# Expert layers: float32 gather and scatter without a second part, the third tile on halves of TensorE, weights in runs of 8 KB

## The chip, the cores and the metric

The program runs on one core of a Trainium2 chip. The metric is the device time of one execution in microseconds (us), of which the kernel before has a median of 965.29 us in three runs (964.44 to 967.16). The traces are of one profiled execution each.

## What is computed

A trunk of two layers runs over 320 tokens of width 1024: 256 of a prompt and 64 of eight samples. Layer 0 has a pooling mixer, layer 1 a sparse attention whose keys and values are projected after layer 0; each layer ends with a mixture of experts. The change is in the experts and in how weights lie in memory. Of 16 experts in 4 groups each token gets 2, of the group that its router picks:

```python
def hmoe(xn, r_group, r_expert, w_gu, w_down):
    ...
    for e in range(N_EXPERTS):
        gu = x2 @ w_gu[e]                                # 1024 x 1024
        hdn = jax.nn.silu(gu[:, :D_EXPERT]) * gu[:, D_EXPERT:]
        y = y + comb[:, e:e + 1] * (hdn @ w_down[e])     # 512 x 1024
```

All weights are float32: 6 MB for an expert, 96 MB for the 16 of a layer.

## The kernel before, in words

The 320 tokens lie in three tiles of 128, 128 and 64 rows (TILE_ROWS) in `H`, the residual stream. Each expert has 64 slots (CAP). Work goes by pairs of experts, 8 pairs to a layer, and by batches of 8 experts (4 pairs), two to a layer.

- `ffn_front` makes the router's tables and the normed rows. ACT writes them rounded to float32r (`copy_high`), DVE the rest that the rounding left (`low_part`, L726): one tile in the front, two at the start of `moe`. The rest of the third tile lies in the upper 64 rows of its high part. At the end PE multiplies constants to stay busy (`keep_streaming`, L217), and all engines meet.
- `gather(b, c)` (L949) is TensorE's: for each of 8 chunks of 128 columns, five products of 512 columns (two parts of tile 0, two of tile 1, one of tile 2 with both parts) against the 0/1 matrix `SG` that DVE builds in one step (L1152). ACT copies each result to `XS` (L1092). Three PSUM banks take turns, and chunk c + 2 follows the gate-up products of step c.
- `gate_up(e)` (L967): 8 steps of 2 products on the two column halves of the array. `turn_hidden` (L981) and `turn_scatter` (L993) transpose; `down(p)` (L1007) has 32 products for the pair, of which the second 16 wait for the last two weight units.
- ACT weighs the product of down by the slots' weights into float32r (`down_high`, L1119), DVE makes what the rounding left (`down_low`, L1174). `scatter(p, m)` (L1033) has six steps of two products (high and low), and DVE adds each to `H` (`add_sums`, L1183). Steps 0 to 3 of pair p lie in the gate-up of the odd expert of the pair behind it, steps 4 and 5 between the two `turn_hidden` of that pair. Of the last pair all six come behind `down`.
- Weights come in units of 1 MB (256 rows), 12 to a pair (8 gate-up, 4 down), 96 to a layer, into a ring of 17. SP issues them in order (`load_unit`, L489), unit n when unit n - 17 was used up. In layer 1, 10 units are loaded long before and 7 at the start of the front. In layer 0 SP waits for the store of a hidden piece (L300) ahead of the unit at 109.87 us. Behind the 96 units of layer 0 come 6 MB of `w_kv` (L913) for the projection (L1407).

One row of a unit is 1024 float32, so one run in memory is 4 KB:

```python
sp.dma_start(M["ring"][:, place_of(layer, n)], src[layer][e, at:at + 2 * P, :].rearrange("(a p) n -> p a n", p=P))
```

Of the kernel before, what the change touches and what calls it, by code (L numbers as in the profile page):

```python
# [14 lines left out]
F32R = mybir.dt.float32r  # L15
# [5 lines left out]
P = 128  # L21
# [421 lines left out]
TURNED = 2 * NE + P  # L443
# [49 lines left out]
def ffn(nc, I, O, M, layer):  # L493

    with ExitStack() as ctx:
        def sb(name, shape, dtype=F32):
# [3 lines left out]
            "comb": sb("weights", [P, NT, NE]), "comb_over": sb("weights_over", [P, NT, NE]),  # L500
            "parts": sb("weight_parts_and_ident", [P, NT, TURNED], F32R), "member": sb("member", [P, NT, NE]),
            "rank": sb("rank", [P, NT, NE]), "list": sb("over_list", [1, 3 * NE]),
            "over": sb("over_ids", [1, MAXOVER + 1], I32),
            "xp": sb("x_parts", [P, 2, NT, D], F32R),
# [7 lines left out]
def ffn_front(nc, I, M, R, layer):  # L512
# [4 lines left out]
    H, XT, ps, stat, XP = M["H"], M["XT"], M["ps"], M["stat"], R["xp"]  # L517
# [5 lines left out]
    with ExitStack() as ctx:  # L523
        sem = lambda n: new_sem(nc, M, f"front{layer}_" + n)
        summed, scaled, rooted, chain = sem("summed"), sem("scaled"), sem("rooted"), sem("chain")
        high, low, turned, by_dve, by_act = (sem("high_ready"), sem("low_ready"), sem("turned"), sem("copied_by_dve"),
                                             sem("copied_by_act"))
# [7 lines left out]
        def _(sp):  # L535
# [12 lines left out]
            sp.wait_ge(high, NT)  # L548

        @block.scalar  # L550
        def _(act):
# [5 lines left out]
            def copy_high(i):  # L557
                r = slice(0, TILE_ROWS[i])
                act.activation(XP[r, 0, i, :], H[r, i, :], ACT.Copy, scale=stat[r, 12 + i:13 + i]).then_inc(high, 1)
# [20 lines left out]
            for i in range(NT):  # L580
                copy_high(i)
# [65 lines left out]
        def _(dve):  # L647
# [60 lines left out]
            low_part(nc, dve, M, R, high, 0, low)  # L708
# [6 lines left out]
            dve.wait_ge(low, 1)  # L715
            st.add(V.tensor_copy(R["total"][0:1, :], ps[3][0:1, 0:NE]))


def low_part(nc, dve, M, R, high, i, done):


    H, XP, stat, rows = M["H"], R["xp"], M["stat"], TILE_ROWS[i]
    if high is not None:
        dve.wait_ge(high, i + 1)
    dst = XP[0:rows, 1, i, :] if i < NT - 1 else XP[NEWTOK:P, 0, i, :]
    nc.vector.scalar_tensor_tensor(dst, H[0:rows, i, :], stat[0:rows, 12 + i:13 + i], XP[0:rows, 0, i, :].bitcast(F32),  # L726
                                   ALU.mult, ALU.subtract).then_inc(done, 1)
# [27 lines left out]
def router_weights(nc, dve, M, R, exp_in, exp_out, ready, listed, chain):  # L755
# [4 lines left out]
    comb, over, rank = R["comb"], R["comb_over"], R["rank"]  # L760
    parts = R["parts"][:, :, 0:2 * NE].rearrange("p i (e x) -> p i e x", x=2)
# [13 lines left out]
    st.add(V.tensor_tensor(comb[:, :, :].rearrange("p i (g e) -> p i g e", g=NG), T["hot1"], T["hot2"], ALU.add))  # L775
    st.add(V.tensor_copy(parts[:, :, :, 0], comb[:, :, :]))
    V.tensor_tensor(parts[:, :, :, 1], comb[:, :, :], parts[:, :, :, 0].bitcast(F32), ALU.subtract).then_inc(ready, 1)

    st.add(V.tensor_scalar(over[:, :, :], rank[:, :, :], float(CAP), None, ALU.is_ge))
    st.add(V.tensor_tensor(over[:, :, :], over[:, :, :], comb[:, :, :], ALU.mult))  # L780
# [27 lines left out]
def moe(nc, I, O, M, R, layer):  # L808
# [5 lines left out]
    H, ps, XP, RW = M["H"], M["ps"], R["xp"], M["ring"]  # L814
# [3 lines left out]
    NM = 2 * NT  # L818
    with ExitStack() as ctx:
# [3 lines left out]
        SG = sb("gather", [P, NT, BATCH * CAP], F32R)  # L823
# [3 lines left out]
        ST = sb("scatter", [P, TOK], F32R)  # L827
        YP = sb("down_parts", [P, 2, 2, FE], F32R)
# [6 lines left out]
        lowest, gT, gi = sem("later_low_ready"), M["gT"], (1, 4)[layer]  # L835
        down_half = sem("down_first_half")
        yh, yl, scattered, added = sem("down_high"), sem("down_low"), sem("scattered"), sem("added")
# [44 lines left out]
        def scatter_bank(p, m):  # L882

            return ps[((5, 7, 5, 7, 5, 7), (5, 7, 0, 1, 5, 7))[p == PAIRS - 1][m]]
# [10 lines left out]
        def _(sp):  # L895
# [23 lines left out]
            def load(k, e):  # L919
                sp.wait_ge(turn, k + 1)  # L920
                sp.dma_start(GU[:, :, :], I["w_gate_up"][layer][bass.ds(e, 1)].rearrange("a (k p) n -> p (a k) n", p=P))\
                    .then_inc(w_in, 16)
                sp.dma_start(DN[:, :, :], I["w_down"][layer][bass.ds(e, 1)].rearrange("a (k p) n -> p (a k) n", p=P))\
                    .then_inc(w_in, 16)
# [11 lines left out]
        def _(pe):  # L936
            def gather(b, c):
                n = KD * b + c
                if c == 0:
                    pe.wait_ge(sg, b + 1)  # L940
                    if b:
                        pe.wait_ge(st_ready, BP * b)
                        pe.wait_ge(ws, 2 * BP * b)
                        pe.wait_ge(added, NM * (BP * b - 1))
                reach(pe, xs, n - 2)
                for part, i in ((0, 0), (1, 0), (0, 1), (1, 1), (0, 2)):
                    if n == 0 and i + part == 2:
                        pe.wait_ge(lowest, i)
                    last = pe.matmul(ps[5 + n % 3][:, 0:BATCH * CAP], XP[:, part, i, c * P:(c + 1) * P],  # L949
                                     SG[:, i, :], start=(part + i == 0), stop=(i == 2))  # L950
                last.then_inc(gathered, 1)

            def gate_up(e, following=None):
                b, x = e // BATCH, e % BATCH
                reach(pe, hid, e - 1)
                if x == 0:
                    for c in range(2):
                        gather(b, c)
                for k in range(KD):
# [14 lines left out]
                    if x == 0 and k + 2 < KD:  # L974
                        gather(b, k + 2)
# [8 lines left out]
            def turn_scatter(p):  # L984
# [7 lines left out]
                for i, rows in enumerate(TILE_ROWS):  # L992
                    last = pe.matmul(ps[6][:, i * TURNED:i * TURNED + 2 * NE + rows], SG[0:rows, i, cols],  # L993
                                     R["parts"][0:rows, i, 0:2 * NE + rows], start=True, stop=True)
                last.then_inc(sturned, 1)

            def down(p):
                pe.wait_ge(ht, 2 * p + 2)
                reach(pe, yl, 2 * p)
# [16 lines left out]
            def scatter(p, m):  # L1016
                t, half = step(p, m)
                rows = TILE_ROWS[t]
                if p == PAIRS - 1 and m == NT:
                    pe.wait_ge(yl, 2 * p + 2)  # L1020
                if m == 0:
                    pe.wait_ge(yl, 2 * p + (2 if p < PAIRS - 1 else 1))
# [3 lines left out]
                    if p == PAIRS - 1:  # L1026
                        pe.wait_ge(hid, NE)
                if p < PAIRS - 1 and m >= 2:
# [11 lines left out]
            for p in range(PAIRS):  # L1040
# [3 lines left out]
                if p:  # L1044
                    scatter(p - 1, 4)
                    scatter(p - 1, 5)
# [36 lines left out]
        def _(act):  # L1083
# [1596 lines left out]
```

## Time and profile before

| | |
|---|---|
| median of three runs | 965.29 us |
| profiled execution | 962.76 us |
| its span | 960.9 us |
| mean granted TensorE clock | 0.985 |
| busy: PE, DVE, ACT | 94%, 36%, 29% of the span |
| DMA, mean over the span | 299 GB/s |
| loads of expert weights | 192 of 1 MB |

A page of the profile gives the busy time of each engine (PE is TensorE, PEld its weight loads), the span in 40 slices of 24 us, the chain of work that ended last, and groups of instructions by line. A product overlaps the one behind it, so its duration is longer than the spacing of products; the chain of waits and the starts in the timeline give the spacing. The timeline gives start and length of runs of instructions, then engine, line, operation, tiles, count, and what an engine was idle for. The views by windows give busy time and counts by engine for a stretch, then the granted clock (1.00 is 2.4 GHz, 0.50 is 1.2 GHz), the share of the 16 DMA engines and GB/s; a share can read a little over 1.

### The profile page before, as it was taken

Reading aid. Unit: us, or ns where it says so; the run is one execution under the profiler, and the core shown is the slowest. Engines: PE = TensorE matmul, PEld = TensorE weight load, DVE = VectorE, ACT = ScalarE, POOL = GpSimd, SP = SyncE. Lnnn points to the kernel's source line nnn. Section 1 sums busy time; section 2 is a strip of 40 time slices with the busy share of each in tenths; the row PEclk is TensorE's granted clock in tenths of the full one; section 3 lists DMA queues with packets and bytes.
Section 4 is the critical chain, followed back from the end, with each engine's and each line's share of the span. In section 5 each row is a group of like instructions: output and inputs, shape, how many; then the busy total and the mean of one; then the engine's idle time right before and its main releaser. Section 6 shows DMA issues by size and latency. Waiting matters only on the chain. (4 is left out here: it accounts for less than half of the span.)

```text
span 960.9 us, 14312 instructions
## 1 busy us (share of the span) xinstructions
PE 899.8 (94%) x5366; PEld 469.8 (49%) x5367; DVE 344.1 (36%) x1022; ACT 275.2 (29%) x611; POOL 29.6 (3%) x112
## 2 busy tenths in 40 slices
PE   4998999999999899999999998699988999999997
PEld 4777433344333444448867665355463333443332
DVE  2244012222222412283255645777344122312223
ACT  2130311121111301141367574556232211111111
POOL 0000000000000000022011100000000000000000
PEclk9998999999999999999999997999998999999999
DMA  9993899999999952546877856290056999999994
GB/s 319 354 410 126 332 409 409 408 409 410 408 409 409 390 192 115 232 176 215 286 252 211 271 190 220 99 409 26 1 219 236 384 409 409 410 409 409 409 408 170
DMA packets 92456, 287.56 MB, mean 299 GB/s; under 512 B 10257, under 2 KB 15761, under 8 KB 91352
## 3 DMA queue, kind: packets, MB, share of 16 engines
q1 hardware_dynamic: 91519, 282.92, 77.7%
q10 hardware_dynamic: 864, 3.67, 1.0%
q8 instruction: 46, 0.75, 0.3%
q14 instruction: 27, 0.21, 0.1%
HBM read 279.55 MB, written 15.50 MB: 307 GB/s over the span
## 5 line engine op out<-in xcount | busy, mean ns | idle before, releaser
L967 PE MATMUL bank<-arena 128*64 128x512 f32 x1024 | 234.9, 600 | 0.0
L967 PEld LDWEIGHTS bank<-arena 128*64 128x64 f32 x1024 | 68.5, 137 | 135.2 <-issue 132.6
L1007 PE MATMUL bank<-arena,moe_hiddenT 128*64 128x512 f32 x512 | 113.6, 596 | 1.9 <-DMA arena<-in_w_down 1.3
L1183 DVE TENSOR_TENSOR residual<-bank,residual 128x512 f32<-128x512 f32 (+1 forms) x96 | 61.4, 682 | 57.5 <-PE bank L1033 57.5
L1160 DVE TENSOR_TENSOR moe_hidden<-moe_silu,bank 128x256 f32<-128x256 f32 x32 | 13.5, 422 | 187.9 <-ACT moe_silu L1097 187.9
L1097 ACT ACTIVATE moe_silu<-bank 128x256 f32<-128x256 f32 x32 | 12.3, 383 | 215.6 <-PE bank L967 215.5
L1007 PEld LDWEIGHTS bank<-arena,moe_hiddenT 128*64 128x64 f32 x512 | 35.6, 137 | 67.9 <-issue 65.3
L288 PE MATMUL bank<-arena 128*128 128x256 f32 x192 | 48.5, 415 | 17.4 <-DMA arena<-in_pages_raw 12.5
L1174 DVE SCALAR_TENSOR_TENSOR moe_down_parts<-bank,moe_slot_weight,moe_down_parts 128x512 fp32r<-128x512 f32 x32 | 24.0, 751 | 96.6 <-ACT moe_down_parts L1119 96.6
L1033 PE MATMUL bank<-moe_down_parts,moe_scatter 128*128 128x512 f32 (+1 forms) x192 | 57.4, 422 | 0.1
L288 PEld LDWEIGHTS bank<-arena 128*128 128x128 f32 x192 | 39.7, 210 | 24.5 <-DMA arena<-in_pages_raw 12.2
L949 PE MATMUL bank<-moe_gather,ffn_x_parts 128*128 128x512 f32 x160 | 47.3, 429 | 3.3 <-DVE moe_gather L1152 2.1
L1119 ACT ACTIVATE moe_down_parts<-bank,moe_slot_weight 128x512 fp32r<-128x512 f32 x32 | 22.0, 687 | 97.3 <-PE bank L1007 97.3
L1033 PEld LDWEIGHTS bank<-moe_down_parts,moe_scatter 128*128 128x128 f32 (+1 forms) x192 | 29.6, 171 | 32.5 <-issue 22.7
L1871 PE MATMUL bank<-upper_b,arena 128*128 128x256 f32 x192 | 45.5, 385 | 0.0
L949 PEld LDWEIGHTS bank<-moe_gather,ffn_x_parts 128*128 128x128 f32 x160 | 28.8, 194 | 31.8 <-ACT arena L1092 17.8
L1407 PE MATMUL bank<-arena,upper_b 128*128 128x512 f32 x96 | 42.0, 596 | 0.1
L1871 PEld LDWEIGHTS bank<-upper_b,arena 128*128 128x128 f32 x192 | 35.1, 191 | 4.9 <-issue 0.4
L1092 ACT ACTIVATE arena<-bank,gainsT 128x512 f32<-128x512 f32 x32 | 22.0, 687 | 47.3 <-PE bank L949 47.3
L1871 PE MATMUL bank<-arena 128*128 128x256 f32 x128 | 32.8, 390 | 0.0
L1689 ACT ACTIVATE arena<-arena 128x256 f32<-128x256 f32 (+1 forms) x64 | 28.3, 444 | 12.3 <-DVE arena L1679 9.3
L1407 PE MATMUL bank<-arena 128*128 128x512 f32 (+1 forms) x96 | 31.2, 486 | 0.0
(328 smaller groups left out, 1042.2 us busy)
## 6 DMA issues: line engine op xcount, KB each, us to landing
arena<-in_w_gate_up SPq DMA_DIRECT2D x128, 1024.0 KB, 18.4
arena<-in_w_down SPq DMA_DIRECT2D x64, 1024.0 KB, 18.6
arena<-in_pages_raw SPq DMA_DIRECT2D x36, 256.0 KB, 4.4
arena<-in_pages_sel SPq DMA_DIRECT2D x32, 256.0 KB, 3.7
upper_b<-in_pages_sel SPq DMA_DIRECT2D x32, 256.0 KB, 3.8
out_new_win_sample<-in_state_win SPq DMA_DIRECT2D x1, 8064.0 KB
arena<-in_w_kv SPq DMA_DIRECT2D x3, 2048.0 KB, 21.0
upper_b<-in_pages_raw SPq DMA_DIRECT2D x24, 256.0 KB, 3.1
```

Source lines behind the costliest of these rows:

```text
L288: last = pe.matmul(at, self.W1[:, kind, half, i, :], rhs, start=(half + i == 0), stop=(half + i == 8), skip_group_check=True)
L949: last = pe.matmul(ps[5 + n % 3][:, 0:BATCH * CAP], XP[:, part, i, c * P:(c + 1) * P], SG[:, i, :], start=(part + i == 0), stop=(i == 2))
L967: last = pe.matmul(ps[e % 2][g * CAP:(g + 1) * CAP, :], XS[:, k, x * CAP:(x + 1) * CAP], w[:, :, g, :], start=(k == 0), stop=(k == KD - 1))
L1007: last = pe.matmul(ps[3 + half][x * CAP:(x + 1) * CAP, :], HT[:, x, c, m * CAP:(m + 1) * CAP], RW[:, place_of(layer, n + x), c, half * 512 ...
L1033: last = pe.matmul(scatter_bank(p, m)[0:rows, :], ST[:, t * P:t * P + rows], YP[:, half, part, :], start=(part == 0), stop=(part == 1))
L1092: A.activation(XS[:, c, :], ps[5 + n % 3][:, 0:BATCH * CAP], ACT.Copy, scale=gT[:, gi, c:c + 1]).then_inc(xs, 1)
L1119: A.activation(YP[:, half, 0, :], ps[3 + half][:, :], ACT.Copy, scale=WS[:, p % 2:p % 2 + 1])\
L1174: V.scalar_tensor_tensor(YP[:, half, 1, :], ps[3 + half][:, :], WS[:, p % 2:p % 2 + 1], YP[:, half, 0, :].bitcast(F32), ALU.mult, ALU.subt ...
L1183: V.tensor_tensor(hv, scatter_bank(p, m)[0:rows, :], hv, ALU.add).then_inc(added, 1)
L1407: last = pe.matmul(bank[:, 0:w], T[:, k, i * P:(i + 1) * P], W[:, k, at:at + w], start=(k == 0), stop=(k == KD - 1))
L1689: act.activation(pp, pp, ACT.Exp, bias=self.sm[:, s, y:y + 1], scale=SCALE, accum_out=self.sm[:, s, 4 + y:5 + y]).then_inc(self.expd, 1)
L1871: last = pe.matmul(at, W1[:, kind, half, i, :], rhs, start=(half + i == 0), stop=(half + i == 8), skip_group_check=True)
```

## The change

- Gather and scatter take the plain float32 values in one product where two of float32r stood. `low_part`, `down_low` and the rounding are gone; DVE and ACT share the weighing of a pair (`weigh_first` for the first 512 columns, `weigh_second`).
- Gather goes by pairs of chunks: two full products for each, then the third tile's 64 rows for both chunks, one on the upper and one on the lower 64 rows of the array. For that the normed third tile is written twice (`norm_rows(NT - 1, NEWTOK)`). Four chunks come ahead of gate-up, pairs follow steps 1 and 3.
- Scatter of the third tile, except for the last pair, is one step with its two column halves side by side; the second lands in the upper 64 rows, is added there and is brought down at the end (`carry`, `merge`).
- `SG` is built in three steps of one tile each, and PE waits for each of them.
- `w_gate_up` and `w_down` are laid out on the host so that a partition's 8 KB of a unit are one run, `w_kv` so that they are runs of 16 KB.

```diff
-TURNED = 2 * NE + P
+TURNED = NE + P
...
     if j < KD:
-        e, at, src = 2 * pair + j // 4, 2 * P * (j % 4), I["w_gate_up"]
+        src = I["gate_up_units"][layer, 2 * pair + j // 4, j % 4]
     else:
-        e, at, src = 2 * pair + j % 2, 2 * P * ((j - KD) // 2), I["w_down"]
-    sp.dma_start(M["ring"][:, place_of(layer, n)], src[layer][e, at:at + 2 * P, :].rearrange("(a p) n -> p a n", p=P))\
-        .then_inc(M["unit_in"][n % RING], 16)
+        src = I["down_units"][layer, 2 * pair + j % 2, (j - KD) // 2]
+    sp.dma_start(M["ring"][:, place_of(layer, n)].rearrange("p a n -> p (a n)"), src).then_inc(M["unit_in"][n % RING], 16)
...
             for i in range(NT):
-                copy_high(i)
+                norm_rows(i)
+            norm_rows(NT - 1, NEWTOK)
...
             V.memset(member[NEWTOK:P, NT - 1, :], 0.0).then_inc(member_in, 1)
-            low_part(nc, dve, M, R, high, 0, low)
+            V.memset(H[NEWTOK:P, NT - 1, 512:D], 0.0).then_inc(upper, 1)
...
-                    sp.dma_start(words[:, at:at + 4096].rearrange("p (k n) -> p k n", k=KD),
-                                 I["w_kv"].rearrange("(k p) n -> p k n", p=P)[:, :, c * 512:(c + 1) * 512]).then_inc(M["kv_in"][c], 16)
+                    sp.dma_start(words[:, at:at + 4096], I["kv_columns"][c]).then_inc(M["kv_in"][c], 16)
...
             def gather(b, c):
+
                 n = KD * b + c
+                if c == 0 and b:
+                    pe.wait_ge(st_ready, BP * b)
+                    pe.wait_ge(ws, 2 * BP * b)
+                    pe.wait_ge(added, NM * (BP * b - 1))
+                for x in range(2):
+                    reach(pe, xs, n + x - 2)
+                    for i in range(NT - 1):
+                        if c + x == 0:
+                            pe.wait_ge(sg, NT * b + i + 1)
+                        pe.matmul(ps[5 + (n + x) % 3][:, 0:BATCH * CAP], XN[:, i, (c + x) * P:(c + x + 1) * P], SG[:, i, :],
+                                  start=(i == 0), stop=False)
                 if c == 0:
-                    pe.wait_ge(sg, b + 1)
-                    if b:
-                        pe.wait_ge(st_ready, BP * b)
-                        pe.wait_ge(ws, 2 * BP * b)
-                        pe.wait_ge(added, NM * (BP * b - 1))
-                reach(pe, xs, n - 2)
-                for part, i in ((0, 0), (1, 0), (0, 1), (1, 1), (0, 2)):
-                    if n == 0 and i + part == 2:
-                        pe.wait_ge(lowest, i)
-                    last = pe.matmul(ps[5 + n % 3][:, 0:BATCH * CAP], XP[:, part, i, c * P:(c + 1) * P],
-                                     SG[:, i, :], start=(part + i == 0), stop=(i == 2))
-                last.then_inc(gathered, 1)
+                    pe.wait_ge(sg, NT * b + NT)
+                for x in range(2):
+                    r = slice(x * NEWTOK, x * NEWTOK + NEWTOK)
+                    pe.matmul(ps[5 + (n + x) % 3][:, 0:BATCH * CAP], XN[r, NT - 1, (c + x) * P:(c + x + 1) * P],
+                              SG[r, NT - 1, :], start=False, stop=True).then_inc(gathered, 1)
...
                 if x == 0:
-                    for c in range(2):
-                        gather(b, c)
+                    gather(b, 0)
+                    gather(b, 2)
...
-                    if x == 0 and k + 2 < KD:
-                        gather(b, k + 2)
+                    if x == 0 and k in (1, 3):
+                        gather(b, k + 3)
...
-                for part in range(2):
-                    last = pe.matmul(scatter_bank(p, m)[0:rows, :], ST[:, t * P:t * P + rows],
-                                     YP[:, half, part, :], start=(part == 0), stop=(part == 1))
+                if p < PAIRS - 1 and t == NT - 1:
+                    for half in range(2):
+                        last = pe.matmul(scatter_bank(p, m)[half * NEWTOK:half * NEWTOK + NEWTOK, :], ST[:, t * P:t * P + rows],
+                                         YW[:, half, :], start=True, stop=True)
+                else:
+                    last = pe.matmul(scatter_bank(p, m)[0:rows, :], ST[:, t * P:t * P + rows], YW[:, half, :],
+                                     start=True, stop=True)
                 last.then_inc(scattered, 1)
...
                 turn_hidden(2 * p)
                 if p:
                     scatter(p - 1, 4)
-                    scatter(p - 1, 5)
                 turn_hidden(2 * p + 1)
...
-            def down_high(p):
+            def weigh_first(p):
                 act.wait_ge(down_half, p + 1)
                 act.wait_ge(ws, 2 * p + 2)
-                reach(act, scattered, NM * p)
-                for half in range(2):
-                    if half:
-                        act.wait_ge(used, UNITS * (p + 1))
-                    A.activation(YP[:, half, 0, :], ps[3 + half][:, :], ACT.Copy, scale=WS[:, p % 2:p % 2 + 1])\
-                        .then_inc(yh, 1)
+                reach(act, scattered, NS * p)
+                A.activation(YW[:, 0, :], ps[3][:, :], ACT.Copy, scale=WS[:, p % 2:p % 2 + 1]).then_inc(y0, 1)
+
+            def carry():
+
+                act.wait_ge(added, NM * (PAIRS - 1))
+                A.copy(SG[0:NEWTOK, 0, :], H[NEWTOK:P, NT - 1, 512:D]).then_inc(carried, 1)
...
-            def down_low(p):
-                for half in range(2):
-                    dve.wait_ge(yh, 2 * p + half + 1)
-                    V.scalar_tensor_tensor(YP[:, half, 1, :], ps[3 + half][:, :], WS[:, p % 2:p % 2 + 1],
-                                           YP[:, half, 0, :].bitcast(F32), ALU.mult, ALU.subtract).then_inc(yl, 1)
+            def weigh_second(p):
+                dve.wait_ge(used, UNITS * (p + 1))
+                dve.wait_ge(ws, 2 * p + 2)
+                reach(dve, scattered, NS * p)
+                V.tensor_scalar(YW[:, 1, :], ps[4][:, :], WS[:, p % 2:p % 2 + 1], None, ALU.mult).then_inc(y1, 1)
...
+            def merge():
+
+                dve.wait_ge(carried, 1)
+                hv = H[0:NEWTOK, NT - 1, 512:D]
+                V.tensor_tensor(hv, SG[0:NEWTOK, 0, :], hv, ALU.add).then_inc(merged, 1)
...
-            for i in range(1, NT):
-                low_part(nc, dve, M, R, None, i, lowest)
...
+    for name in ("gate_up", "down"):
+        w = x["w_" + name]
+        arrays[name + "_units"] = w.reshape(2, NE, -1, 2, P, D).transpose(0, 1, 2, 4, 3, 5).reshape(2, NE, -1, P, 2 * D)
+    arrays["kv_columns"] = x["w_kv"].reshape(KD, P, 3, 512).transpose(2, 1, 0, 3).reshape(3, P, KD * 512)
```

## Rows read from the trace of the kernel before

**Rows 1.** The page: busy us by engine; then GB/s in 40 slices of 24 us.
```profile
PE 899.8 (94%) x5366; PEld 469.8 (49%) x5367; DVE 344.1 (36%) x1022; ACT 275.2 (29%) x611; POOL 29.6 (3%) x112
...
GB/s 319 354 410 126 332 409 409 408 409 410 408 409 409 390 192 115 232 176 215 286 252 211 271 190 220 99 409 26 1 219 236 384 409 409 410 409 409 409 408 170
```
**Rows 2.** Windows, expert stages: busy us by engine, then clock, DMA share, GB/s.
```profile
112.00:318.00 206.00, 204.56 (x917) 77.66 (x913) 48.54 (x89) 33.03 (x73) 0.00 (x0) 1.00 1.02 409
...
750.00:944.00 194.00, 193.17 (x866) 73.71 (x862) 47.64 (x86) 30.04 (x67) 0.00 (x0) 1.00 1.02 406
944.00:946.00 2.00, 1.99 (x10) 0.78 (x12) 0.49 (x3) 0.49 (x2) 0.00 (x0) 1.00 0.09 37
```
**Rows 3.** Timeline, layer 0's last `down`, second 16 products: start, us, what, idle before.
```profile
318.73 3.65 PE L1007 MATMUL bank<-arena,moe_hiddenT 128*64 128x512 f32 x16 [1.34 <-DMA arena<-in_w_down]
```
**Rows 4.** DMA view, 429 to 432 us: packets with their sizes, and rate.
```profile
DMA packets 170, 1.26 MB, mean 421 GB/s; under 512 B 16, under 2 KB 16, under 8 KB 16
```
**Rows 5.** Windows, 30 to 33 us, the DMA engines full with mixed sizes.
```profile
30.00:33.00 3.00, 3.00 (x16) 2.60 (x16) 0.00 (x0) 0.85 (x2) 0.00 (x0) 1.00 1.07 379
```
**Rows 6.** Chain of work, layer 1, second batch and next pair: start, us, what.
```profile
837.86 2.53 PE bank L949 x10
840.39 1.01 PE bank L967 x4
841.40 1.36 PE bank L949 x5
...
875.00 7.72 PE bank L967 x36
```
**Rows 7.** Timeline, weight loads of the projection's full-width float32 products.
```profile
332.26 0.19 PEld L1407 LDWEIGHTS bank<-arena,upper_b 128*128 128x128 f32 x1 [0.24 <-issue]
332.69 0.19 PEld L1407 LDWEIGHTS bank<-arena,upper_b 128*128 128x128 f32 x1 [0.24 <-issue]
```
**Rows 8.** Timeline: float32 products on row halves, then on column halves.
```profile
603.53 1.13 PE L1661 MATMUL bank<-arena 64*128 64x512 f32 x4
...
754.63 7.09 PE L1007 MATMUL bank<-arena,moe_hiddenT 128*64 128x512 f32 x32
```
**Rows 9.** Timeline, layer 1, between gate-up and `down` of the second pair.
```profile
778.08 0.38 ACT L1097 ACTIVATE moe_silu<-bank 128x256 f32<-128x256 f32 x1 [9.07 <-PE bank L967]
...
778.50 0.42 DVE L1160 TENSOR_TENSOR moe_hidden<-moe_silu,bank 128x256 f32<-128x256 f32 x1 [2.33 <-ACT moe_silu L1097]
...
779.18 0.38 PE L981 MATMUL bank<-constants,moe_hidden 128*128 128x128 f32 x2
```
**Rows 10.** Timeline, the start of layer 1's experts.
```profile
721.47 1.76 DVE L1152 TENSOR_TENSOR moe_gather<-constants,ffn_rank 128x1536 fp32r<-128x1536 f32 x1 [3.35 <-PEq L523]
...
723.28 1.31 PE L949 MATMUL bank<-moe_gather,ffn_x_parts 128*128 128x512 f32 x3 [2.11 <-DVE moe_gather L1152]
...
726.12 2.92 PE L949 MATMUL bank<-moe_gather,ffn_x_parts 128*128 128x512 f32 x6 [0.51 <-DVE ffn_x_parts L726]
...
728.97 1.84 PE L967 MATMUL bank<-arena 128*64 128x512 f32 x4
```
**Rows 11.** Chain of work, layer 1: the end of expert 0, all of expert 1.
```profile
744.05 8.76 PE bank L967 x40
```
**Rows 12.** Windows, around the router of layer 1 and at the experts' start.
```profile
703.60:711.00 7.40, 3.92 (x41) 2.86 (x41) 4.02 (x9) 5.14 (x9) 0.62 (x1) 1.00 0.65 221
...
723.70:730.50 6.80, 6.08 (x14) 2.58 (x12) 5.85 (x23) 1.69 (x4) 0.00 (x0) 0.50 0.81 320
```
**Rows 13.** Timeline, the last pair of layer 1, behind `down`.
```profile
951.17 0.69 ACT L1119 ACTIVATE moe_down_parts<-bank,moe_slot_weight 128x512 fp32r<-128x512 f32 x1 [1.05 <-PE bank L1007]
951.89 0.75 DVE L1174 SCALAR_TENSOR_TENSOR moe_down_parts<-bank,moe_slot_weight,moe_down_parts 128x512 fp32r<-128x512 f32 x1 [0.99 <-ACT moe_down_parts L1119]
952.56 3.67 DVE L1183 TENSOR_TENSOR residual<-bank,residual 128x512 f32<-128x512 f32 x6
```
**Rows 14.** Timeline, one DVE step of 128 x 512 out of SBUF.
```profile
42.95 0.69 DVE L396 TENSOR_TENSOR residual<-residual,upper_a 128x512 f32<-128x512 f32 x1
```

More of the change, by code:

```diff
@@ L525, in ffn_front @@
         summed, scaled, rooted, chain = sem("summed"), sem("scaled"), sem("rooted"), sem("chain")
-        high, low, turned, by_dve, by_act = (sem("high_ready"), sem("low_ready"), sem("turned"), sem("copied_by_dve"),
-                                             sem("copied_by_act"))
+        normed, turned, by_dve, by_act = sem("rows_normed"), sem("turned"), sem("copied_by_dve"), sem("copied_by_act")
+        upper = sem("upper_rows_cleared")
         columns, lt_ready = sem("logit_columns_ready"), sem("logit_columns_copied")
@@ L547, in _ @@
             sp.wait_ge(spilled, 16)
-            sp.wait_ge(high, NT)
+            sp.wait_ge(normed, NT + 1)
+            sp.wait_ge(upper, 1)
         @block.scalar
@@ L555, in square_rows, with norm_rows @@
                 act.wait_ge(summed, n + 1)
-            def copy_high(i):
+            def norm_rows(i, at=0):
                 r = slice(0, TILE_ROWS[i])
-                act.activation(XP[r, 0, i, :], H[r, i, :], ACT.Copy, scale=stat[r, 12 + i:13 + i]).then_inc(high, 1)
+                act.activation(XN[at:at + TILE_ROWS[i], i, :], H[r, i, :], ACT.Copy, scale=stat[r, 12 + i:13 + i])\
+                    .then_inc(normed, 1)
             def copy_turned(i):
@@ L714, in _ @@
             dve.wait_ge(ranks, 2)
-            dve.wait_ge(low, 1)
             st.add(V.tensor_copy(R["total"][0:1, :], ps[3][0:1, 0:NE]))
[L719 to L727, printed above, removed]
 def router_tables(R):
@@ L808, in moe @@
 def moe(nc, I, O, M, R, layer):
-    H, ps, XP, RW = M["H"], M["ps"], R["xp"], M["ring"]
+    H, ps, XN, RW = M["H"], M["ps"], R["xn"], M["ring"]
     ident, slots = const(M, "ident"), const(M, "slots")
@@ L826, in moe @@
         HT = sb("hiddenT", [P, 2, 2, P])
-        ST = sb("scatter", [P, TOK], F32R)
-        YP = sb("down_parts", [P, 2, 2, FE], F32R)
+        ST = sb("scatter", [P, TOK])
+        YW = sb("down_weighted", [P, 2, FE])
         WS = sb("slot_weight", [P, 2])
@@ L882, in scatter_bank @@
         def scatter_bank(p, m):
-            return ps[((5, 7, 5, 7, 5, 7), (5, 7, 0, 1, 5, 7))[p == PAIRS - 1][m]]
+            return ps[((5, 7, 5, 7, 5, 5), (5, 7, 0, 1, 5, 7))[p == PAIRS - 1][m]]
         def step(p, m):
@@ L920, in load @@
                 sp.wait_ge(turn, k + 1)
[L921 to L924, printed above, removed]
+                for w, src in ((GU, I["gate_up_units"]), (DN, I["down_units"])):
+                    sp.dma_start(w[:, :, :].rearrange("p (u k) n -> p u (k n)", k=2),
+                                 src[layer][bass.ds(e, 1)].rearrange("a u p n -> p (a u) n")).then_inc(w_in, 16)
             def over_ended():
@@ L992, in turn_scatter @@
                 for i, rows in enumerate(TILE_ROWS):
-                    last = pe.matmul(ps[6][:, i * TURNED:i * TURNED + 2 * NE + rows], SG[0:rows, i, cols],
-                                     R["parts"][0:rows, i, 0:2 * NE + rows], start=True, stop=True)
+                    last = pe.matmul(ps[6][:, i * TURNED:i * TURNED + NE + rows], SG[0:rows, i, cols],
+                                     R["table"][0:rows, i, 0:NE + rows], start=True, stop=True)
                 last.then_inc(sturned, 1)
@@ L1137, in _ @@
                 copy_scatter(p)
-                down_high(p)
+                if p == PAIRS - 1:
+                    carry()
+                weigh_first(p)
             def over_expert(k, e):
@@ L1199, in _ @@
                     build_gather((p + 1) // BP)
-                down_low(p)
+                if p == PAIRS - 1:
+                    merge()
+                weigh_second(p)
             def over_expert(k, e):
```

77 lines of the change are left out of this document (42 added, 35 removed).

## The prediction

> **What bounds the kernel now.** I read the page first, then the windows of the expert stages, the timeline at the last `down` of each layer, the chain of waits and the timeline at each place that the diff touches. The page says PE is busy 94% of the span, which points at TensorE; its GB/s slices stand at 409 for all of both expert stages, which points at the DMA engines [rows 1]. The windows show both at once: over 206 us of layer 0 PE is busy for 204.6 and the DMA share is full, and so in layer 1 [rows 2]. So the question is which runs out first at the end of a layer. In layer 0 PE stands 1.34 us for `in_w_down` ahead of its last 16 products [rows 3]: the weights are late. In layer 1 loading falls to 37 GB/s only from 944 to 946 [rows 2], and the products that need those units start at about 951.1 - 3.65 = 947.5 ([rows 3] for the 3.65, [rows 13] for the end): weights are early by 1.4 us. The two streams are even to within 1.4 us in each layer, though PE alone is faster for most of the way: a ring of 17 units, full at the start, is eaten up exactly by the end. A change that makes only one of them faster wins next to nothing in layer 0, so both halves of this change have to be priced.
>
> **The part on the weights: runs of 8 KB.** Today runs of 4 KB give 409 GB/s [rows 2]. A place with larger runs is 429 to 432 us: of 170 packets only 16 are under 8 KB, and the rate is 421 [rows 4]. I take 421, since sizes and direction are the same. That shortens the stream by 1 - 409/421 = 2.9%: 0.029 x 206 = 5.9 us in layer 0 and 0.029 x 194 = 5.6 in layer 1. Bounds: no gain (409) above, and below a loss to 379, the rate of full DMA engines with mixed sizes [rows 5]. Layer 0's last units then land at 318.7 - 5.9 = 312.8. The same runs for `w_kv` save some us of transfers behind the last unit; the projection does not wait for them now, and they stay ahead of it, so I count nothing.
>
> The Trainium skill ("DMA: Bandwidth & Descriptors", Why small descriptors are slow) puts a fixed cost of about 3 cycles on a packet that moves 32 bytes a cycle. For 4 KB and 8 KB that is 131/128 against 259/256, an estimate of 1.1%, so about 414 GB/s and not 421. It is a rival below.
>
> **TensorE, unit prices.** Ten float32r products take 2.53 us and five 1.36 [rows 6], so one is 0.234 and the entry into another form of the array 0.19. A return to gate-up costs 0.15: 4 products take 1.01, while 36 take 7.72, or 0.2145 each [rows 6]. A plain float32 product of full width comes every 0.43 us [rows 7]: dearer than one float32r, cheaper than two (0.468). Two on row halves start together, and four take 1.13, which is 2 x 0.43 and the entry; column halves give 7.09/32 = 0.22 [rows 8]. So two halves cost 0.43 together.
>
> **Gather.** A batch has 8 chunks. Before: 2.53 for the first two, 6 x 1.36 for the others, 7 returns of 0.15, in all 11.7 us. After: four pairs, each with four full products and two halves, 5 x 0.43 = 2.15, and two entries (full, then halves) of 0.19, so 2.53 a pair; with three returns 10.6 us. Saving 1.15 a batch, and the halves' entries have eaten half of it. ACT's copies (0.69) hide under the eight gate-up products between pairs.
>
> **Scatter in the middle pairs, 7 a layer.** Steps 0 to 3 lie within gate-up: four plain products for eight rounded ones, 4 x (0.468 - 0.43) = 0.15. Steps 4 and 5 become one step of two halves, 0.43 for 0.94. But what is late next? The second `turn_hidden` starts at 779.18 today, and its input comes from ACT at 778.08 + 0.38 and DVE at 778.50 + 0.42 = 778.92 [rows 9], so it can start at 778.97. Of 0.5 us only 0.21 are won. Sum 0.36 a pair, 7 x 0.36 = 2.5 us a layer.
>
> **Start of the experts, layer 1.** Today DVE builds `SG` in 1.76 us, PE starts at 723.28, stops for the two `low_part` and reaches gate-up at 728.97; the clock is 0.50 from 723.7 to 730.5 [rows 10, 12]. Expert 0 ends at 744.05 + 0.15 + 8 x 0.2145 = 745.9 [rows 11]. After: a third of `SG` takes 0.69, as a step of that size does [rows 14], so PE starts at 722.2, the later tiles are ready by 722.8 and 723.4, and nothing stops it. The clock is the choice. PE stood 2.11 us before it fell [rows 10]; now it stands 1 us. Around the router PE is busy for only 3.92 of 7.4 us, in pieces, and the clock holds at 1.00 [rows 12]. A gap of 1 us behind a run of constants and in front of solid work is nearer to that, so I take 2.4 GHz. Then: two pairs until 727.4 (0.15 for waits on `SG`), two steps of gate-up 1.87, a pair 2.53, two steps 1.87, a pair 2.53, four steps 3.58: expert 0 ends at 739.8, 6.1 us earlier. In layer 0 the gather follows a long piece of hidden work of PE, so there only the 1.15 of the batch counts. `norm_rows`' extra call, `memset` and the DVE's shorter tables lie in the front, beside PE's constants.
>
> **Tail, both layers.** Behind the last `down` DVE waits for ACT (951.17 + 0.69), makes the low part (0.75) and then adds six times, so the adds start at 952.65 [rows 13]. After, the first half is weighed within `down`, DVE weighs the second from 951.17 to 951.87, PE's first scatter is done by 951.1 + 0.19 + 0.43 = 951.7 with its drain some 0.1 later, and the adds start at 951.9. Saving 0.75. `carry` and `merge` lie inside the 7 us of `down`.
>
> **New waits.** PE's waits on `y1` and SP's on `normed` and `upper` queue nothing that is not long ready; SP's ring waits (`used`) come earlier with PE.
>
> **The sum**, from the profiled execution of 962.76 us (span 960.9, and 1.9 around it). Layer 0: stall 1.34 + gathers 2.3 + scatters 2.5 = 6.1, and the last 16 products would start at 312.6; weights land at 312.8, so 5.9. Layer 1: start 6.1 + second gather 1.15 + scatters 2.5 = 9.8, so PE is there at 937.7; weights, which start with the ring's first free unit 6 us earlier, land at 946.1 - 6.1 - 5.6 = 934.4 and hide. Tails 1.5. In all 17.2: 945.6 for a profiled execution. The median stands 2.5 above it: 965.29 - 17.2 = 948.1 us, with 945.5 to 950.5 for this case alone. The rest of the program (attention, projection) only shifts.
>
> **Rivals.**
> - The clock still falls at layer 1's start. The front work would then lie in 6.8 us at half speed: 1.35 us of it done by 723.7, 3.4 by 730.5, gate-up from 730.8, expert 0 done at 743.3, only 2.6 us earlier. For it: it fell there today. Price 3.5: 951.6.
> - Runs of 8 KB bring only 1.1% by a fixed cost per packet: streams 2.3 and 2.1 us shorter. Layer 0's units land at 316.4 and save 2.3 for 5.9; layer 1's at 937.9, still about PE's time. 951.9. Against it stands the 421 of [rows 4]. The Trainium skill's "DMA: Bandwidth & Descriptors" is its source.
> - They bring nothing, TensorE alone gains: layer 0 saves none of the 5.9, layer 1 lands at 940.0 and saves 7.5 of 9.8. Total 9.0: 956.3. For it: [rows 4] is 3 us of other loads.
> - Halves do not run side by side in these places: 16 pairs of chunks x 0.43 and 14 scatters x 0.24: 10.3 us, 958.4. Against it [rows 8].
> - Slower than before: an 8 KB run occupies its DMA engine for longer than two of 4 KB, and the stream, not PE, sets the end of both layers. At 379 GB/s [rows 5] it is 7.9% longer: 16.3 and 15.4 us. Layer 0 loses 16.3; layer 1 loses 15.4 - 6.1 - 1.4 = 7.9; less tails, 22.7 in all: 988. It decides against the change from about 401 GB/s down (2.2% of 400 us is the 9 us of the rest). Against it: the 421.
>
> **How the numbers follow.** Forecast 0.45, clock 0.2, 1.1% 0.08, no DMA gain 0.12, serial halves 0.05, slower DMA 0.05, and 0.05 for a larger gain than I see (944). The range runs from 943.5 to 957: it takes in the first four cases and the larger gain, 0.9, and leaves out serial halves and slower DMA. A change of 0.3% is 2.9 us, about what can be told from none. All cases but slower DMA save over that: faster 0.93, same 0.02, slower 0.05.
>
> **What would show it.** DMA at 421 over 112 to 310 us, and no wait for `in_w_down` beyond 0.5 us. Gate-up of pair after pair 0.15 shorter, `turn_hidden` 0.2 closer, a gather pair at 2.5 us. Layer 1: PE from 722.2 relative to the same front, clock 1.00, expert 0 done 18 us after the experts' start (24 today). The six adds start 0.75 us behind the last `down`. Wrong if the DMA share is full at 409 or less, if PE waits for weights in layer 1, or if full-width products in the gather are further apart than 0.43.

## The result: 5.7% slower, and the profile after

| | before | after |
|---|---|---|
| median | 965.47 us (4 runs) | 1022.86 us (4 runs) |
| ratio of after to before | | 1.057, interval 1.052 to 1.063 |
| profiled execution, its span | 962.76, 960.9 us | 1025.05, 1023.2 us |
| mean granted TensorE clock | 0.985 | 0.980 |

The quotient of the two medians is 1.059, inside the interval. The forecast was 948.1 us, and it missed by 75 us and in sign. The page of after: busy us by engine; GB/s in 40 slices of 25.6 us; then groups by line with count, busy us and mean ns.

```profile
PE 967.5 (95%) x5446; PEld 474.4 (46%) x5447; DVE 332.0 (32%) x1008; ACT 266.4 (26%) x599; POOL 29.8 (3%) x112
...
GB/s 308 373 405 151 293 423 420 419 419 339 375 420 405 92 220 88 224 143 242 297 206 224 270 147 200 228 273 1 32 308 212 422 419 419 419 323 394 419 217 53
...
L958 PE MATMUL bank<-arena 128*64 128x512 f32 x1024 | 230.6, 596 | 0.0
...
L1029 PE MATMUL bank<-moe_down_weighted,moe_scatter 128*128 128x512 f32 (+1 forms) x136 | 67.4, 618 | 0.0
...
L935 PE MATMUL bank<-moe_gather,ffn_x_normed 128*128 128x512 f32 x128 | 59.2, 605 | 1.5 <-DVE moe_gather L1151 1.0
```

PE has more to do than before, 967.5 us for 899.8 [rows 1], with 80 more matmul instructions, though the code issues fewer products. The weights stream at 419 to 420 GB/s where it was 409, and now they are the ones that wait: slices at 339, 375 and 323 lie inside the expert stages. TensorE is the bound, and by far.

The chain of waits at layer 1's start shows where it goes (start, us, what), two pairs of chunks and the first steps of gate-up:

```profile
757.35 0.70 DVE moe_gather L1151
...
758.10 3.70 PE bank L935 x8
761.80 1.06 PE bank L941 x4
762.86 3.63 PE bank L935 x8
766.49 1.06 PE bank L941 x4
767.55 1.87 PE bank L958 x8
```

L935 holds the full products of a pair of chunks. The loops issue four of them (two tiles, two chunks); the trace has **eight instructions** in 3.63 us. L941 issues two half products and shows four instructions. A pair costs 4.69 us, where I had forecast 2.53. The weight loads of one such pair, one for each instruction, stand 0.43 us apart:

```profile
763.76 0.19 PEld L935 LDWEIGHTS bank<-moe_gather,ffn_x_normed 128*128 128x128 f32 x1 [0.24 <-issue]
764.18 0.19 PEld L935 LDWEIGHTS bank<-moe_gather,ffn_x_normed 128*128 128x128 f32 x1 [0.24 <-ACT arena L1087]
```

So 0.43 us is the price of an instruction, and a plain float32 product of 512 columns is two of them: 0.86 us, against 0.234 for a float32r product. The Trainium skill ("FP8 and Floating Point Precision", TensorE Precision Notes) says that true FP32 takes 4 passes through the array; four times 512 columns at 2.4 GHz would be 0.853 us, an estimate, and the trace agrees with its two times 0.43. I did not weigh that rule, and it spoke against this change.

A middle pair of layer 1, in the chain of after from gate-up to `down`:

```profile
827.87 7.72 PE bank L958 x36
835.60 1.91 PE bank L1029 x4
837.51 3.58 PE bank L958 x16
841.10 1.91 PE bank L1029 x4
843.01 2.73 PE bank L958 x12
845.74 0.37 PE bank L972 x2
846.10 1.01 PE bank L1026 x4
847.11 0.37 PE bank L972 x2
847.48 0.87 PE bank L984 x6
```

The same stretch of before, which the forecast's rows did not show:

```profile
820.22 1.13 PE bank L1033 x4
821.34 3.58 PE bank L967 x16
824.93 1.12 PE bank L1033 x4
826.05 2.73 PE bank L967 x12
828.78 0.37 PE bank L981 x2
829.15 0.95 PE bank L1033 x4
830.10 0.22 PE bank L981 x2
830.31 0.43 PE bank L993 x3
```

Two scatter steps: 1.91 for 1.13, twice. The third tile: 1.01 for 0.95. The second `turn_hidden`: 0.37 for 0.22; it now follows products on both column halves, and 0.37 is what the first one takes behind gate-up in both kernels. `turn_scatter` (L984, before L993): six instructions in 0.87 for three in 0.43, because its table and `SG` became float32 too. That is 2.2 us, against the 2.1 between the starts of two `down`s (27.5 us after, 25.4 before): `down` itself follows at once and takes 7.02 us for 7.09, so 0.1 of the 0.44 comes back.

**A table of stages**, for this and all runs below. A stage is, in the timeline, from the first product of a layer's first gather to the end of its last `down`; the middle is what lies between the two stages, with layer 0's tail, attention and the front.

| profiled run | layer 0 | middle | layer 1 | median against before |
|---|---|---|---|---|
| before | 225.4 | 400.9 | 227.8 | 1 |
| after | 253.9 | 409.2 | 253.9 | 1.057 (1.052 to 1.063) |
| rounded_gather | 227.0 | 404.1 | 227.3 | 1.005 (1.003 to 1.007) |
| plain_gather | 241.5 | 407.9 | 241.5 | 1.040 (1.038 to 1.043) |
| plain_scatter | 236.4 | 404.3 | 239.8 | 1.031 (1.029 to 1.032) |
| one_half | 260.8 | 402.5 | 260.8 | 1.077 (1.070 to 1.085) |
| runs8_only | 223.9 | 400.9 | 227.8 | 0.998 (0.995 to 1.001) |
| after_runs4 | 253.9 | 405.2 | 253.9 | 1.057 (1.053 to 1.062) |
| paired | 221.1 | 401.0 | 221.3 | 0.987 (0.982 to 0.991) |
| paired_runs4 | 225.4 | 403.9 | 221.5 | 0.994 (0.991 to 0.998) |
| high_only_8 | 220.3 | 408.7 | 218.6 | 0.994 (0.991 to 0.997) |
| high_only_4 | 225.7 | 411.4 | 221.9 | 1.010 (1.005 to 1.016) |

The ratios are to runs of before taken beside each kernel (median 963.6 us from rounded_gather on, 963.7 for the last two). After against before: 28.5 + 26.1 in the stages and 2 x 1.4 in the tails make 57.4, the difference of the medians. The two profiled executions differ by 62.3: what lies ahead of layer 0's stage is 2.0 us shorter in after, and its middle is another 6.9 us longer, with 34 us at half clock where before has 14. The middle, which but for layer 0's tail, the `w_kv` layout and the front's table building and rows is the same code, varies by 10.5 us between profiled runs, in part with its stretches at half clock (10 to 34 us), so I compare stages.

### The profile page after: what moved, and what is told of

The parts are those of the page before. It is cut to its first block and busy times, and to the rows that moved or that the text cites. A ratio compares the mean times of both kernels' runs of the same rounds, so it can differ in the third digit from the quotient of the medians.

```text
span 1023.2 us, 14477 instructions
## 1 busy us (share of the span) xinstructions
PE 967.5 (95%) x5446; PEld 474.4 (46%) x5447; DVE 332.0 (32%) x1008; ACT 266.4 (26%) x599; POOL 29.8 (3%) x112
## 5 line engine op out<-in xcount | busy, mean ns | idle before, releaser
L958 PE MATMUL bank<-arena 128*64 128x512 f32 x1024 | 230.6, 596 | 0.0
L1189 DVE TENSOR_TENSOR residual<-bank,residual 128x512 f32<-128x512 f32 (+1 forms) x96 | 66.3, 691 | 86.1 <-PE bank L1029 78.1
L1159 DVE TENSOR_TENSOR moe_hidden<-moe_silu,bank 128x256 f32<-128x256 f32 x32 | 13.5, 422 | 228.7 <-ACT moe_silu L1092 228.7
L1029 PE MATMUL bank<-moe_down_weighted,moe_scatter 128*128 128x512 f32 (+1 forms) x136 | 67.4, 618 | 0.0
L935 PE MATMUL bank<-moe_gather,ffn_x_normed 128*128 128x512 f32 x128 | 59.2, 605 | 1.5 <-DVE moe_gather L1151 1.0
L1029 PEld LDWEIGHTS bank<-moe_down_weighted,moe_scatter 128*128 128x128 f32 (+1 forms) x136 | 22.4, 186 | 44.3 <-issue 42.8
L1175 DVE TENSOR_SCALAR moe_down_weighted<-bank,moe_slot_weight 128x512 f32<-128x512 f32 x16 | 12.0, 751 | 91.9 <-PE bank L999 91.9
L935 PEld LDWEIGHTS bank<-moe_gather,ffn_x_normed 128*128 128x128 f32 x128 | 23.0, 189 | 36.4 <-issue 26.4
L1111 ACT ACTIVATE moe_down_weighted<-bank,moe_slot_weight 128x512 f32<-128x512 f32 x16 | 11.0, 687 | 75.9 <-PE bank L999 75.9
## 6 DMA issues: line engine op xcount, KB each, us to landing
arena<-in_gate_up_units SPq DMA_DIRECT2D x128, 1024.0 KB, 12.4
arena<-in_kv_columns SPq DMA_DIRECT2D x3, 2048.0 KB, 12.4
```

The lines of the kernel that those rows point to most:

```text
L935: pe.matmul(ps[5 + (n + x) % 3][:, 0:BATCH * CAP], XN[:, i, (c + x) * P:(c + x + 1) * P], SG[:, i, :], start=(i == 0), stop=False)
L958: last = pe.matmul(ps[e % 2][g * CAP:(g + 1) * CAP, :], XS[:, k, x * CAP:(x + 1) * CAP], w[:, :, g, :], start=(k == 0), stop=(k == KD - 1))
L1159: V.tensor_tensor(HR[:, e % 2, :], SIL[:, e % 2, :], ps[e % 2][:, FH:], ALU.mult).then_inc(hid, 1)
L1189: V.tensor_tensor(hv, scatter_bank(p, m)[at:at + rows, :], hv, ALU.add).then_inc(added, 1)
```

## Experiments

Theory 1: a plain float32 product is two instructions. Theory 2: it costs 0.43 us, and the time lies in the new order, array forms or waits. Theory 3: 8 KB runs slow the weights.

### rounded_gather: one type changed

```diff
-            "xn": sb("x_normed", [P, NT, D]),
+            "xn": sb("x_normed", [P, NT, D], F32R),
-        SG = sb("gather", [P, NT, BATCH * CAP])
+        SG = sb("gather", [P, NT, BATCH * CAP], F32R)
```

The table of weights goes with them, and `carry` uses a buffer of its own.

> The changed kernel with its tables, the normed rows and the gather matrix in float32r instead of float32: the order, the pairs of chunks and the row halves stay, the low parts stay away, so the gathered rows are rounded to float32r (that remainder is left out). Theory 1 (a plain float32 product of 512 columns is two instructions of 0.43 us, a float32r one is one of 0.234): a pair of chunks falls from 4.69 us to 5 x 0.234 + 2 x 0.19 = 1.55, four pairs in four batches save 50 us, turn_scatter gives 0.43 x 16 = 7 us: about 966 us. Theory 2 (the type is not it; the new order, with four chunks ahead and two entries of array forms a pair, costs the time): at most 0.2 us a product comes back, 80 products, 16 us: above 1000 us. Theory 3 (8 KB runs slow the weights): stays within 3 us of 1023.

Measured 968.2 us. The chain of waits at one pair of chunks, followed by two steps of gate-up:

```profile
732.53 1.12 PE bank L938 x4
733.64 0.43 PE bank L944 x2
734.08 1.87 PE bank L961 x8
```

With the same products in the same order, instructions halve (x4 for x8, x2 for x4) and the pair falls from 4.69 to 1.55 us, the number that theory 1 gave. Theories 2 and 3 expected over 1000. The median came down from 1022.9 to 968.2, by 54.7 us (50 by the two ratios); 57 was expected. Layer 0's stage gave 27.0 of the 28.5 expected.

### plain_gather and plain_scatter: each half alone

plain_gather keeps the scatter of before in the changed kernel; plain_scatter is the kernel before with the layout and the changed scatter:

```diff
-        ST = sb("scatter", [P, TOK], F32R)
-        YP = sb("down_parts", [P, 2, 2, FE], F32R)
+        ST = sb("scatter", [P, TOK])
+        YW = sb("down_weighted", [P, 2, FE])
```

> The changed gather, tables and layout, with the scatter of the kernel before (float32r, high and low parts). Theory 1: the batches cost 7.5 us more in each of four, of which the start of layer 1 gives back about 5; turn_scatter costs 0.43 to 0.55 us more in each of 16 pairs; the stall for weights in layer 0 (1.34) goes: 965.4 + 25 + 8 - 1.3 = 997 us. Theory 2 (a product costs 0.43 and the loss lies in the scatter and its waits): 955 to 963. Theory 3 (the weights are slow): near 1023.

> The changed scatter and the layout, with the gather and tables of the kernel before. Theory 1: scatter steps cost 1.55 us more in each of 14 middle pairs, 1.45 more in each tail, less the stall of 1.34: 965.4 + 21.7 + 2.9 - 1.3 = 988.7 us. With plain_gather's excess it adds up to that of the changed kernel (57). Theory 2 (a product costs 0.43, the loss is in the gather): 958 to 963. Theory 3: near 1023.

Measured 1001.6 and 993.7 us. Both are slower than before, by 38 and 30 us, more than the 32 and 23 of theory 1; theory 2 had each under 963. In the profiled runs the middle is 7.0 and 3.4 us longer than before. In plain_gather it has 27 us at half clock for before's 14, and a stop of 3.7 us. In plain_scatter 1.5 of the 3.4 are layer 0's tail; its half clock is 14 us as in before, and the other 1.9 us stay open. The profiled run of plain_scatter is also its fastest (988.0 us, mean clock 0.988), and the others, at 992.2 to 994.6, show 0.975 to 0.982. The stage of layer 0 is clean: over runs8_only (223.9), gather adds 17.6 us and scatter 12.5, together 30.1, and the changed kernel stands 30.1 above it. Scatter follows from the rows above: 2 x 0.78 + 0.06 + 0.15 = 1.77 a pair, seven pairs, 12.4. Gather: 2 x 7.5 for the batches (19.2 us for 11.7), and 8 times what `turn_scatter` costs. Its own 0.44 would make 18.5, 0.9 too much; but plain_gather has 25.70 us between the starts of two `down`s where before has 25.37 (805.40 and 830.77), so only 0.33 a pair is left of it, and the sum is 17.6, as measured.

### one_half: are row halves concurrent?

```diff
-                    r = slice(x * NEWTOK, x * NEWTOK + NEWTOK)
+                    r = slice(0, NEWTOK)
```

> The changed kernel with both products of the gather's third tile on rows 0 to 63, so they can't lie side by side. The lower rows hold the same numbers as the upper ones, so the result is the same. If halves of rows do run side by side, each of 16 pairs of chunks costs 2 x 0.43 = 0.86 us more: 1023 + 13.8 = 1037 us. If they are served one after the other anyway, it stays at 1023.

```profile
776.02 1.91 PE bank L941 x4
777.93 1.87 PE bank L958 x8
```

Two half products on the same rows take 1.91 us, on different rows 1.06 (chain of waits, both). Layer 0's stage grew by 6.8, eight pairs by 0.86 being 6.9. The whole took 1034.1 us, where 1037 was expected. So the halves did run side by side; this step of the forecast held, and "serial halves" falls.

### runs8_only and after_runs4: the layout alone, and taken away

```diff
-        e, at, src = 2 * pair + j // 4, 2 * P * (j % 4), I["w_gate_up"]
+        src = I["gate_up_units"][layer, 2 * pair + j // 4, j % 4]
```

> The kernel before with the new layout of the weights alone (8 KB runs). Theory 1 (the stream rises from 409 to 420 GB/s, but TensorE sets the pace except for its 1.34 us at the end of layer 0): 1.3 us off, 962.3 where before gives 963.6; no wait of TensorE for weights is left. Theory 3 (longer runs hold up the stream): slower, by up to 23 us.

> The changed kernel with the old layout (4 KB runs, 409 GB/s). Theory 1: TensorE is 28 us a layer slower than the stream needs, so the layout is hidden: the same as the changed kernel, ratio 1.057, stage of layer 0 at 253.9 us. Theory 3 (the weights cost the time): clearly faster than it, down to 1.0.

The kernel before with 8 KB runs: 961.5 us, ratio 0.998 with an interval that includes 1; its layer 0 is 1.6 us shorter and PE waits for no weights there. The changed kernel with 4 KB runs: 1020.9, ratio 1.057 and stages to within 0.1 us those of the changed kernel. Theory 3 falls at both ends: the layout costs nothing, and where TensorE is 28 us a layer too slow it also brings nothing.

### paired and paired_runs4: what was of use in the change

The kernel before keeps its float32r products. It takes the gather in pairs of chunks, `SG` in three steps, and the low parts of tiles 1 and 2 move into the front; paired has the 8 KB layout as well.

```diff
-                    for c in range(2):
+                    for c in range(4):
                         gather(b, c)
...
-                    if x == 0 and k + 2 < KD:
-                        gather(b, k + 2)
+                    if x == 0 and k in (1, 3):
+                        gather(b, k + 3)
+                        gather(b, k + 4)
...
+            for i in range(1, NT):
+                low_part(nc, dve, M, R, high, i, low)
+            dve.wait_ge(low, NT)
```

> The kernel before with all that the change had of use and without its float32 products: 8 KB runs, the gather in pairs of chunks (four ahead, the others behind steps 1 and 3 of gate-up), its table built in three steps, and the low parts of tiles 1 and 2 made in the front and not at the start of the experts. Products stay float32r with high and low parts. Batches save 3 returns of 0.15 each and up to 2 entries, layer 1 starts about 5 us earlier if the clock then stays at 2.4 GHz, the stall of 1.34 goes: 3 to 11.6 us off, 952 to 960.6 where before gives 963.6. If the low parts in the front are on its path, 1.5 us a layer of this are lost.

> The same with the old layout (4 KB runs). If the layout is what lets a faster TensorE count, the gain in layer 0 disappears here (the stream ends as before) and layer 1 keeps only its slack of 1.4 us and its earlier start: 3 to 6 us more than the version with 8 KB runs. If the stream was no bound, both are equal.

paired: **952.7 us, ratio 0.987 (0.982 to 0.991)**, faster than both kernels. Its chain at layer 1's start:

```profile
718.72 0.70 DVE moe_gather L1153
...
719.46 5.20 PE bank L948 x20
724.66 1.87 PE bank L966 x8
726.53 2.54 PE bank L948 x10
```

The gather runs without a stop, 2.5 us for two chunks with both parts, and the granted clock stays 1.00:

```profile
719.00:745.00 26.00, 24.97 (x107) 11.81 (x108) 8.70 (x38) 9.07 (x15) 0.00 (x0) 1.00 0.82 303
```

In before it was 0.50 from 723.7 to 730.5 [rows 12]. The same split goes through all the kernels: the five that keep the gather of before with its stops (before, runs8_only, plain_scatter and the two of the last experiment) fell to 0.50 within 3.5 us of PE's start in layer 1, and the seven that start without a stop stayed at 1.00 there. Layer 1's stage gives 6.5 us. In layer 0 paired gives 4.4 and paired_runs4 exactly nothing: 225.4 both. The profiled run of paired_runs4 takes 958.3 us, 5.6 more than that of paired, where 3 to 6 was expected. Its timeline shows why; PE is early and stands for the weights four times from 296.8 us on, 3.4 us in all, the last time as in [rows 3]:

```profile
317.41 3.65 PE L1010 MATMUL bank<-arena,moe_hiddenT 128*64 128x512 f32 x16 [1.50 <-DMA arena<-in_w_down]
```

The layout alone brings 1.6 us in layer 0, the faster TensorE alone 0, and both together 4.4: this is the shape I had predicted for two even streams.

### high_only_8 and high_only_4: the stream by itself

```diff
-                for part, i in ((0, 0), (1, 0), (0, 1), (1, 1), (0, 2)):
+                for part, i in ((0, 0), (0, 1), (0, 2)):
...
-                for part in range(2):
+                for part in range(1):
```

> The kernel before with 8 KB runs and without the products of the low parts in gather and scatter (the remainders that rounding to float32r leaves of the normed rows and of the down outputs are left out). TensorE is some 9 us a layer faster and must wait for the weights, so the stream alone sets the stages. If 8 KB runs give 2.9% more, the stage of layer 0 (225.4 us before) goes to about 219.5, 5.9 us below that of the version with 4 KB runs; in all some 944 us. If they gave 1.1% it would be 2.3 us below, if nothing, equal.

> The same with the old layout (4 KB runs, 409 GB/s); the same remainders are left out. The stream is full from the start and sets the end: the stage of layer 0 stays at 225 us though TensorE has 9 us less to do; layer 1 gains its earlier start and its slack of 1.4 us: some 955 us. Theory 3 (longer runs hold up the stream) would make this one the faster of the two.

Windows of 160 to 300 us, in high_only_8 and then in high_only_4 (busy us and count by engine, clock, DMA share, GB/s):

```profile
160.00:300.00 140.00, 133.39 (x583) 45.50 (x583) 35.22 (x63) 22.23 (x48) 0.00 (x0) 1.00 1.01 420
```

```profile
160.00:300.00 140.00, 132.51 (x565) 45.34 (x565) 33.78 (x61) 21.85 (x47) 0.00 (x0) 0.98 1.02 409
```

PE has gaps and the DMA engines none: the stream sets the stage. Layer 0 takes 220.3 against 225.7 us, 5.4 between them where 5.9 was forecast and a fixed cost of 1.1% would give 2.3. My sum of the work left out was too low (32 products of the gather and 42 of the scatter, by 0.234, are 17 us a layer, not 9), but it could not matter: with 4 KB the stage ends where it ended before. The rule of the Trainium skill that made the 1.1% ("DMA: Bandwidth & Descriptors", Why small descriptors are slow) disagrees with this: 420 against 409 GB/s is 2.7%. The section also names 32 bytes of descriptor data for each operation, which the 1.1% left out; with them it is 1.5%, an estimate, and still short of what was measured.

The totals missed, 957.4 for 944 and 973.4 for 955: **less work made the kernel with 4 KB runs slower than before.** Behind some waits for a unit the clock was low. High_only_4 in the timeline at one `down`, and the window behind it:

```profile
252.76 4.82 PE L1007 MATMUL bank<-arena,moe_hiddenT 128*64 128x512 f32 x14 [1.46 <-DMA arena<-in_w_down]
```

```profile
252.60:256.00 3.40, 3.24 (x8) 1.13 (x10) 0.00 (x0) 0.00 (x0) 0.00 (x0) 0.50 1.03 411
...
327.80:341.30 13.50, 6.87 (x23) 5.66 (x24) 2.82 (x5) 3.45 (x6) 0.00 (x0) 0.50 0.67 232
```

Such falls go with three waits of 1.46 and 1.47 us in this stage, and high_only_8, with waits of up to 1.35, kept 1.00 through it. But paired_runs4 also kept 1.00 behind its wait of 1.50 above, so the length of the wait alone does not decide, and that the waits are the cause is not shown. Inside the stage these falls are hidden by the stream. Behind it more is lost: at layer 0's end PE stood still from 326.4 to 333.1 ahead of its constants, 6.65 us (before: 0.69), the clock fell to 0.50 in that standstill, at 327.8, and came back at 341.3:

```profile
333.07 2.93 PE L217 MATMUL bank<-constants 128*128 128x256 f32 x6 [6.65 <-issue]
```

The profile names no releaser for these 6.65 us. They stand in high_only_8 as well (6.55) and in part in plain_gather (3.71); the other runs have 1.5 at most there, and only these three show half clock at this place. One view of high_only_4 points at PE's own code. From 327 to 333 us the DMA engines are full with other loads, and of the instruction queue q8 there is one packet, of 16 KB, that ends at 331.6 (q8 is taken for PE's, since its packets go with the number of PE's instructions: 45 here, 46 in before, 47 in after):

```profile
q1 hardware_dynamic: 1130, 2.27, 102.4%
q8 instruction: 1, 0.02, 1.1%
```

In each of the seven runs where PE stood over 1.1 us here, its first constant product comes 1.40 to 1.49 us behind the end of such a packet of this queue; in the other five the distance is anything from 0.03 to 6.9 us. So PE probably waited for instructions. No run varies this, and the cause is not shown.

## Why the prediction was wrong

- **The failed step: "A plain float32 product of full width comes every 0.43 us [rows 7]: dearer than one float32r, cheaper than two (0.468)."** I read the spacing of instructions in [rows 7] and took it for the spacing of products. It is 0.86. The rows could have told me: the chain has L967 x4 for one step of gate-up [rows 6], and such a step issues two products; the page of before, below, has 1024 of them for 512. [rows 6] also has L949 x5 for five float32r products. I divided once by products and once by instructions and compared the two. My own sign of being wrong (full products further apart than 0.43) had the same flaw: the weight loads of after still stand 0.43 apart.

```profile
L967 PE MATMUL bank<-arena 128*64 128x512 f32 x1024 | 234.9, 600 | 0.0
```

- The same slip sits in [rows 8]: "four take 1.13, which is 2 x 0.43" were two products, not four. Being on both sides, it confirmed the wrong price.
- **Gather**, forecast 1.15 saved a batch: 7.5 lost. Four pairs at 4.69 + 3 x 0.15 are 19.2. With 0.86 in the forecast's own sum (4.3 and two entries of 0.19) a pair would have been 4.68.
- **Scatter**, forecast 0.36 saved a pair: 1.77 lost, by the same price. The cap by `turn_hidden`'s input never counted, since PE itself was late.
- **`turn_scatter`** I had not priced at all. Its operands change type as well: 0.44 a pair by itself, 0.33 after what `down` gives back, about 5 us in all. Unlike the first point, this is an omission in the list of what the edit touches.
- **Start of layer 1.** The choice of 2.4 GHz was right: after shows 1.00 over 757 to 785, and paired turns it into time. One of its reasons was weak: the clock does not always hold around the router, and in after it was 0.50 from 744.1 to 750.9, in front of the experts. PE's row of products without a stop was right too. Expert 0 was done 26.9 us after the experts' start, where 18 was forecast; the four pairs' excess of 2.16 each is 8.6 of these 8.9.
- **Tail**, forecast 0.75 saved: the first add starts 1.09 us behind the last `down` (before 1.46), so the earlier weighing gave 0.37. Then each add waits for a product of 0.86, and the tail takes 6.55 for 5.13.
- **Weights.** 421 GB/s forecast, 419 to 420 measured; 5.9 us forecast, 5.4 in the pair of kernels that the stream bounds. The 1.1% rival and "no gain" fall, and so does the slower one: it ended on the right side, by a mechanism that does not exist here. The stall of 1.34 went, as forecast, because TensorE came later.
- **The range and the chances.** None of my cases varied the price of the product; all varied what I had already called uncertain. The price of the one operation that the change is made of rested on one row, without a bound above. It should have had one, from the count.

## What to carry to other kernels

Before a duration is multiplied, hold the instruction count of its group against the products that the loops issue: here 1024 for 512. By that a plain float32 product costs 0.86 us for 512 columns, so splitting into a high and a low float32r part (0.47) is nearly twice as fast, and worth its extra steps on DVE and ACT. And where TensorE and the weights are even, price both halves together: 0 and 1.6 us alone were 4.4 us together.

## What the runs showed of the hardware that I had not expected

- Plain float32 is two instructions a product in the trace, float32r one; the same loops gave x128 and x64 when only the type changed (L935 of after, L938 of rounded_gather):

```profile
L935 PE MATMUL bank<-moe_gather,ffn_x_normed x128: 592/592/697, 95.0 to 903.7; 128*128 128x512 f32 x128
```

```profile
L938 PE MATMUL bank<-moe_gather,ffn_x_normed x64: 388/397/503, 95.6 to 847.9; 128*128 128x512 f32 x64
```

- With 17 us a layer less for TensorE to do, high_only_4 ended 1.0% above before: its stage of layer 0 was bound by the weights and won nothing, and behind it stood 6.65 us of standstill and 13.5 us at half clock. What ties the two together is not shown.
- The clock at the start of layer 1 went with the stops: 0.50 in all five kernels with them, 1.00 in all seven without.
- Two float32r products on different row halves start together like float32 ones: 0.43 for both, entry included, in rounded_gather.
